# A fused diffusion step on one core: feed-forward in blocks of 128 inner columns with six PSUM banks for the down product, third modulation group summed on VectorE

## The reference, cut to what matters

```
D_MODEL = 1024; D_FF = 2816
def swiglu(h, w_gu, w_down):
    g, u = jnp.split(h @ w_gu, 2, axis=-1)
    return (jax.nn.silu(g) * u) @ w_down

x = x + g2 * swiglu(modulate(rmsnorm(x, norm2_g_0), s2, sc2), w_gu_0, w_down_0)
```

```
m = jax.nn.silu(cond.astype(F32)) @ w.astype(F32) + b.astype(F32)     # w: 1024 x 6144
```

## Time and profile before

| what | value |
|---|---|
| median of 3 runs | 1412.44 us (1411.51 to 1413.75) |
| profiled execution, first to last instruction (span) | 1408.6 us, which is 3.8 us under the median; no other time is given for it |
| PE / DVE / ACT busy | 96% / 79% / 58% of the span |
| mean granted TensorE clock | 0.986 of full speed |
| feed-forward, first gate matmul to last residual add | 254.4 to 539.9 us |

### The profile page before, as it was taken

How to read it: one execution, slowest core, us unless ns; L and a number is a source line. 1 busy time by engine, 2 the same in 40 slices (tenths; PEclk the granted TensorE clock), 3 DMA queues, 4 the chain that set the end, 5 groups by cost and what they waited for, 6 DMA issues and landing times.

```text
span 1408.6 us, 17000 instructions
## 1 busy us (share of the span) xinstructions
PE 1351.2 (96%) x6717; PEld 1126.3 (80%) x6717; DVE 1117.5 (79%) x1031; ACT 811.1 (58%) x812; POOL 238.1 (17%) x338
## 2 busy tenths in 40 slices
PE   4999989999999998989999999999999999999996
PEld 2787557799999986788888888888888888888884
DVE  2698766567676656658899899998998999989997
ACT  4432764423232224255777777777777777767773
POOL 4000681000000013001999200000000000000001
PEclk9999999999999999989999999999999999999998
DMA  9967444854554437537899999999999999999991
GB/s 312 378 228 268 134 144 163 312 196 151 180 179 163 166 147 245 196 135 290 288 401 388 363 412 371 381 388 355 414 375 372 412 348 397 386 355 406 369 413 53
DMA packets 119238, 409.75 MB, mean 291 GB/s; under 512 B 8385, under 2 KB 31090, under 8 KB 102258
## 3 DMA queue, kind: packets, MB, share of 16 engines
q1 hardware_dynamic: 111376, 382.24, 72.2%
q0 software_dynamic: 6704, 23.14, 5.4%
q10 hardware_dynamic: 1074, 3.23, 0.6%
HBM read 398.58 MB, written 9.99 MB: 290 GB/s over the span
## 4 chain that ended last, share of the span: by engine, by line
PE 88%; POOL 4%; DVE 3%; DMA 2%; ACT 1%; issue 1%; SPq 1%; POOLq 0%; DVEq 0%; ACTq 0%
PE ps L1814 26%; PE ps L1816 26%; PE ps L1815 26%; DMA raw<-in_ada_w 2%; PE ps L2196 1%; POOL xn L725 1%; POOL o_rstd L723 1%; DVE ring_lo L1612 1%; PE ps L2096 1%; POOL o_msq L721 1%; PE ps L2038 1%; PE ps L2139 1%; SPq L502 1%; PE ps L2169 1%; DMA gbc<-in_cache_v 0%
## 5 line engine op out<-in xcount | busy, mean ns | idle before, releaser
L1612 DVE TENSOR_TENSOR ring_lo<-raw,ring_hi 128x2048 fp32r<-128x2048 f32 (+1 forms) x210 | 451.9, 2168 | 49.2 <-ACT ring_hi L1048 48.5
L1048 ACT ACTIVATE ring_hi<-raw 128x2048 fp32r<-128x2048 f32 (+1 forms) x210 | 381.3, 1820 | 123.8 <-PE ps L1816 122.8
L1814 PE MATMUL ps<-ring_hi,xe 128*128 128x512 f32 x536 | 212.1, 396 | 1.3 <-DVE xe L1663 0.8
L1816 PE MATMUL ps<-ring_lo,xe 128*128 128x512 f32 x536 | 209.8, 391 | 0.0
L1815 PE MATMUL ps<-ring_hi,xe 128*128 128x512 f32 x536 | 209.3, 390 | 0.0
L824 ACT ACTIVATE ring_hi<-raw 128x2048 fp32r<-128x2048 f32 x52 | 99.3, 1914 | 168.3 <-PE ps L1816 156.1
L1192 DVE TENSOR_TENSOR ring_lo<-raw,ring_hi 128x2048 fp32r<-128x2048 f32 x52 | 118.2, 2288 | 83.6 <-ACT ring_hi L824 83.4
L1612 DVE TENSOR_TENSOR ring_lo_more<-raw,ring_hi_more 128x2048 fp32r<-128x2048 f32 (+1 forms) x70 | 151.8, 2168 | 16.7 <-ACT ring_hi_more L1048 16.5
L1048 ACT ACTIVATE ring_hi_more<-raw 128x2048 fp32r<-128x2048 f32 (+1 forms) x70 | 127.3, 1819 | 40.1 <-PE ps L1816 39.7
L1814 PEld LDWEIGHTS ps<-ring_hi,xe 128*128 128x128 f32 x536 | 101.4, 189 | 21.9 <-DVE xe L1663 0.9
L1816 PEld LDWEIGHTS ps<-ring_lo,xe 128*128 128x128 f32 x536 | 101.0, 188 | 21.5
(11 more groups left out here) (325 smaller groups left out, 2428.8 us busy)
## 6 DMA issues: line engine op xcount, KB each, us to landing
raw<-in_w_gu_e SPq DMA_DIRECT2D x128, 1024.0 KB, 8.1
raw<-in_w_down_e SPq DMA_DIRECT2D x88, 1024.0 KB, 9.0
raw<-in_w_gu_e SPq DMA_DIRECT2D x64, 768.0 KB, 6.9
raw<-in_ada_w SPq DMA_DIRECT2D x40, 1024.0 KB, 5.5
raw<-in_w_gu SPq DMA_DIRECT2D x44, 512.0 KB, 4.9
raw<-in_w_qkv SPq DMA_DIRECT2D x12, 1024.0 KB, 8.1
raw<-in_w_down SPq DMA_DIRECT2D x11, 1024.0 KB, 5.2
raw<-in_ada_w SPq DMA_DIRECT2D x16, 512.0 KB, 13.6
```

The lines of the kernel that those rows point to most:

```text
L1048: act.activation(ehi[m % RINGM][:, 0:w], raw[:, (MOE_U0 + m) % RAW, 0:w], ACT.Copy).then_inc(hi_ready, 1)
L1612: dve.tensor_tensor(elo[m % RINGM][:, 0:w], raw[:, (MOE_U0 + m) % RAW, 0:w], ehi[m % RINGM][:, 0:w].bitcast(F32), ALU.subtract).then_inc(l ...
L1814: pe.matmul(out, l_hi, r_hi, start=first, stop=False)
L1816: return pe.matmul(out, l_hi, r_lo, start=False, stop=last)
```

## The change

- The feed-forward goes in 22 blocks of 128 inner columns (`BLOCKS`). Two blocks share the three weight units of a chunk. A block's gate goes to bank 6 and its up to bank 7, 48 matmuls of 384 columns; then follows the down product of the block before, 18 matmuls of 512 columns.
- The six outputs of the down product have a bank each, 0 to 5, and are summed there over all 22 blocks. `add_y`, `yacc` and the 66 additions on DVE are gone; `add_gated` reads PSUM.
- PE must wait, before each block's gate and up, until DVE has read those of the block before (`ffh_ready`), and now works one down product of 18 matmuls in between.
- Group 3 is summed on DVE like groups 1 and 4 (`FOLDED`), in blocks 1 to 8, and group 4 in blocks 11 to 18 (`FOLD_FFN`). Their rows are summed on PE behind blocks 9 and 19, and turned behind 10 and 20. The `ada_unit` calls of group 3 are gone.
- `STREAM` and the split order on ACT and DVE follow the new order.

```diff
+BLOCKS = 2 * FFC
+FOLD_FFN = {1 + i: (3, i) for i in range(KC)} | {11 + i: (4, i) for i in range(KC)}
+SUM_AFTER = {9: 3, 19: 4}
+TURN_AFTER = {10: 3, 20: 4}
-FOLDED = (1, 4)
+FOLDED = (1, 3, 4)
...
+            for b in range(BLOCKS):                                    # ACT
+                c, at = b // 2, b % 2
+                if at:
+                    act.wait_ge(unit_used, FFN0 + 3 * c + 2)
+                else:
+                    act.wait_ge(gu_ps, c + 1)
+                if b >= 2:
+                    act.wait_ge(ffh_ready, b - 1)
+                act.activation(tnh[:, at, :], ps[:, 6, 0:TOK], ACT.Tanh, scale=0.5).then_inc(tanh_ready, 1)
+                act.wait_ge(ffh_ready, b + 1)
+                act.activation(ff_hi[:, at, :], hb[:, at, :], ACT.Copy).then_inc(ffhi_ready, 1)
+                if at == 0:
+                    split_hi(FFN0 + 3 * c + 2)
+                if c + 1 < FFC:
+                    split_hi(FFN0 + 3 * c + 3 + at)
...
+            for b in range(BLOCKS):                                    # DVE
+                c, at = b // 2, b % 2
+                dve.wait_ge(tanh_ready, b + 1)
+                link(dve.scalar_tensor_tensor(hb[:, at, :], tnh[:, at, :], 1.0, ps[:, 6, 0:TOK], ALU.add, ALU.mult))
+                dve.scalar_tensor_tensor(hb[:, at, :], hb[:, at, :], 0.5, ps[:, 7, 0:TOK],
+                                         ALU.mult, ALU.mult).then_inc(ffh_ready, 1)
+                dve.wait_ge(ffhi_ready, b + 1)
+                dve.tensor_tensor(ff_lo[:, at, :], hb[:, at, :], ff_hi[:, at, :].bitcast(F32),
+                                  ALU.subtract).then_inc(fflo_ready, 1)
+                if at and c + 1 < FFC:
+                    split_lo(FFN0 + 3 * c + 4)
+                if b in FOLD_FFN:
+                    fold_in(*FOLD_FFN[b])
+                if b in SUM_AFTER:
+                    ada_rows_out(SUM_AFTER[b])
+                if b in TURN_AFTER:
+                    ada_cols_out(TURN_AFTER[b])
+                if at == 0:
+                    split_lo(FFN0 + 3 * c + 2)
+                    if c + 1 < FFC:
+                        split_lo(FFN0 + 3 * c + 3)
...
-            turn_normed(1, lambda k: ada_unit(3, k) if k < 2 else None)
-            for k in range(2, KC - 2):
-                ada_unit(3, k)
+            turn_normed(1)
...
+            def add_down(b):
+                c, at = b // 2, b % 2
+                slot = (FFN0 + 3 * c + 2) % RING
+                pe.wait_ge(fflo_ready, b + 1)
+                pe.wait_ge(lo_ready, FFN0 + 3 * c + 3)
+                for k in range(TILES):
+                    cols = slice(k * P, (k + 1) * P)
+                    for half in range(2):
+                        w = slice(at * D + half * HALF, at * D + (half + 1) * HALF)
+                        ins = mm3(ps[:, 2 * k + half, :], ff_hi[:, at, cols], ff_lo[:, at, cols],
+                                  ring_hi[:, slot, w], ring_lo[:, slot, w], b == 0, b == BLOCKS - 1)
...
+            for b in range(BLOCKS):                                    # PE
+                if b:
+                    pe.wait_ge(ffh_ready, b)
+                    gate_up(b, 0)
+                gate_up(b, 1)
+                if b:
+                    add_down(b - 1)
+                if b in SUM_AFTER:
+                    pe.wait_ge(ffh_ready, b + 1)
+                    fold_unit(SUM_AFTER[b])
+                if b in TURN_AFTER:
+                    pe.wait_ge(ffh_ready, b + 1)
+                    ada_turn(TURN_AFTER[b])
+            add_down(BLOCKS - 1)
```

More of the change, by code:

```diff
@@ L97, in stream_before_experts @@
     s += wo[1:]
[L98 to L104, removed]
+    s += DENSE_UNITS[:2]
+    for b in range(BLOCKS):
+        c = b // 2
+        later = DENSE_UNITS[3 * c + 3:3 * c + 5]
+        fold = [("ada",) + FOLD_FFN[b]] if b in FOLD_FFN else []
+        s += later[1:] + fold if b % 2 else fold + [DENSE_UNITS[3 * c + 2]] + later[:1]
     s += [("ada", 5, k) for k in range(KC)]
@@ L115 @@
 FFN0 = WO0 + 4
-WF0 = FFN0 + NU
+WF0 = FFN0 + len(DENSE_UNITS)
 MOE0 = WF0 + 4
@@ L286, in dense @@
             with ExitStack() as q:
-                ff_hi = sb("ff_hi", [P, 2, 2, TOK], F32R, q)
-                ff_lo = sb("ff_lo", [P, 2, 2, TOK], F32R, q)
+                ff_hi = sb("ff_hi", [P, 2, TOK], F32R, q)
+                ff_lo = sb("ff_lo", [P, 2, TOK], F32R, q)
                 tnh = sb("tnh", [P, 2, TOK], F32, q)
@@ L2033, in _ @@
                     pe.wait_ge(hlo_ready, 12)
-                for q in range(4):
-                    for b in range(4):
-                        w = q * HALF + (b % 2) * 256 + (b // 2) * P
+                for up in range(2):
+                    for q in range(4):
+                        w = q * HALF + up * 256
                         for weight in weights:
-                            ins = pe.matmul(ps[:, b, 0:TOK], weight[:, FFN0 % RING, w:w + P], part[:, q, :],
-                                            start=(q == 0 and part is h_hi and weight is ring_hi), stop=False)
@@ new lines, in _, with gate_up @@
+                            pe.matmul(ps[:, 6 + up, 0:TOK], weight[:, FFN0 % RING, w:w + P], part[:, q, :],
+                                      start=(q == 0 and part is h_hi and weight is ring_hi), stop=False)
+            def gate_up(b, kh):
+                c, at = b // 2, b % 2
+                slot = (FFN0 + 3 * c + kh) % RING
+                pe.wait_ge(lo_ready, FFN0 + 3 * c + kh + 1)
+                for up in range(2):
+                    if up and kh == 0 and b - 1 in SUM_AFTER:
+                        pe.wait_ge(mrow_ready, SUM_AFTER[b - 1] + 2)
+                    if up and kh == 0 and b - 1 in TURN_AFTER:
+                        pe.wait_ge(modv_ready, TURN_AFTER[b - 1] + 2)
+                    for q in range(4):
+                        w = q * HALF + up * 256 + at * P
+                        ins = mm3(ps[:, 6 + up, 0:TOK], ring_hi[:, slot, w:w + P], ring_lo[:, slot, w:w + P],
+                                  h_hi[:, 4 * kh + q, :], h_lo[:, 4 * kh + q, :], kh == 0 and q == 0, kh == 1 and q == 3)
+                if at:
+                    ins.then_inc(unit_used, 1)
+                elif kh:
+                    ins.then_inc(gu_ps, 1)
```

120 lines of the change are left out of this document (22 added, 98 removed).

## The result

| | before | after |
|---|---|---|
| median | 1411.97 us (1410.95 to 1413.75, 4 runs) | 1419.54 us (1419.09 to 1420.38, 4 runs) |
| ratio | | 1.0053, interval 1.004 to 1.0066 |
| span of the profiled execution | 1408.6 us | 1417.6 us |
| mean granted clock | 0.986 | 0.979 |

The changed kernel is slower by 0.53%, 7.6 us by the medians and 9.0 us by the two spans. The forecast was 1416.6 us in a range from 1412.9 to 1420.8; the sign and the range held, and the time lies 2.9 us over the forecast. The kernel before came out at 1411.97 us here where the forecast had started from 1412.44, so as a difference the miss is larger: +7.6 us in place of +4.2, a little over the forecast's own upper bound of +7.2.

A forecast was written before the change was run, and what follows sets the result against it. The prediction took PE to bound the feed-forward, so relieving DVE saves nothing by itself. Its terms, +0.45 - 1.05 + 2.05 + 0 + 2.0 + 0.8 = +4.2 us on 1412.44, gave 1416.6 us, range 1412.9 to 1420.8.

The forecast's parts named there:

- gap behind the first block: Between the first two blocks, PE idles 2.0 us in place of 3.07, as the `ada_unit`s are gone: -1.05 us.
- `fold_unit(3)`: Group 3's row sum, new inside PE's chain in the feed-forward: 26.91 us a chunk against 24.86, +2.05 us.
- twice as many switches: PE changes between gate-and-up and down products twice as often: +0.45 us, at most 0.9.
- end of the feed-forward, without the clock: Behind the last down product, earlier last add (-0.1 to -0.4) set against PE free about 0.3 us late: 0.
- clock at the entrance: Before the first gate matmul, PE idles 5.4 us and then runs at its lower clock: +2.0 us (1.5 to 2.5).
- clock at the end: Behind the feed-forward, PE's gap grows from 2.88 to about 4.2 us; half the lower price of 1.5 to 2.5: +0.8.
- The bound: The feed-forward is bound by PE, busy 278.7 of 279.8 us; work leaving DVE gives no time back by itself.
- The schedule: Feed-forward blocks: 2.0 us idle between the first two, a tanh every 12.4 us, no other PE waits; +1.0 to +1.9.
- The clock holds: Rival: no added clock loss at the feed-forward's entrance or end, only schedule, 1413.4 to 1414.4 us; chance 0.26.
- A late split: Rival: PE stalls for late splits in odd blocks, +5, with the clock 1422 us; both kinds, about 1438; chance 0.12.
- A faster pitch: Rival: down product's 512-column pitch shrinks to 0.2133 us without DVE reading banks beside it, 1408.6 us; chance 0.06.

The follow-up runs named there:

- three gaps filled: Changed kernel plus unused identity transposes on idle PE: 36 at the feed-forward's entrance, 15 between the first two blocks, 30 at the end; 1.0017 of the kernel before.
- second trace of the changed kernel: The changed kernel profiled again with no edit; ratio 1.0039 to the kernel before, span 1414.0 us.
- blocks alone, filled: Changed kernel with group 3 back on PE, plus 15 unused transposes between the first two blocks and 30 at the end; 1.0004 of the kernel before.
- second trace of before: The kernel before profiled again with no edit; ratio 0.9999, span 1411.2 us.
- two gaps filled: Changed kernel plus unused identity transposes on idle PE, 36 at the feed-forward's entrance and 30 at its end; 1.0023 of the kernel before.
- a third kernel: Kernel before plus unused transposes: 16 before the first head's turn, 36 before the last attention output's, 24 at the feed-forward's end; 0.9986 of the kernel before.
- the kernel before with all places filled: Kernel before plus unused transposes at five places: 16, 36 and 24 as in the third kernel, 15 more at the feed-forward's entrance; ratio 0.9993.

## Why the prediction was right, and which term was off

Both columns are us against the kernel before. The measured ones for the schedule come from the traces of the changed kernel and of three gaps filled, where the clock was at full, and those for the clock from the first and second trace of the changed kernel less that one.

| step | predicted | measured |
|---|---|---|
| gap behind the first block | -1.05 | 1.92 - 3.07 = -1.15 |
| `fold_unit(3)` | +2.05 | (392.61 - 378.11) - 12.47 = +2.03 |
| twice as many switches | +0.45 (0 to 0.9) | +0.8, what is left of +1.70 |
| end of the feed-forward, without the clock | 0 | 11.86 - 11.89 = 0 |
| clock at the entrance | +2.0 (1.5 to 2.5) | +1.68 and +2.45 |
| clock at the end | +0.8 | 14.49 and 13.30 less 11.86: +2.6 and +1.4 |
| sum | +4.2 | +6.0 and +5.6 |

**The bound** was read rightly: 66 additions left DVE and no time came back (blocks alone, filled: 1.0004).

**The schedule** came out as worked: the gap is 1.92 us where 2.0 were said, a tanh follows every 12.47 us where 12.4 were, PE waits for nothing else, and the first residual multiply starts 540.66 - 538.21 = 2.45 us ahead of the end of the down product where before it was 534.02 - 527.48 = 6.54, 4.1 nearer; the last add ends 8.06 us behind it, like 12 operations. The switches cost near their upper bound: ACT's timeline shows 0.07 us a pair of blocks, which is 0.8 over eleven.

**The clock at the entrance** behaved as said, and filling the gap took its price away (1.67 us). How much it costs depends on the execution. The Trainium skill, "TensorE: Matmul & The Clock Gate", Part 1: The HAM clock gate, says that the number of slow matmuls differs between runs of one kernel; the two traces of the changed kernel agree, with 1.68 and 2.45 us.

**The clock at the end is the mis-sized term**: "I take half of the lower price, +0.8." The gap was right (4.07 for 4.2), but the halving was not: in all four traces in which the blocks' end stood unfilled the clock fell, for 1.4 to 2.6 us (11.86 the measure), and in neither trace of before did it. My reason for halving, that before might pay it already behind 2.88 us, has no trace for it at this place; at the first head the clock did fall behind gaps of 2.81 and 2.85 us, so the length of a gap alone does not tell. With the mean of the two traces of the changed kernel, 2.0, the forecast would have been 1417.8; the two comparisons gave +7.6 and +5.9 us by the medians (1418.67 - 1412.77 the second).

**What remains** is 0.3 to 1.6 us between the measured sums and the differences of the medians, and the close agreement of the second is partly luck: its trace is the shortest of five executions. There the feed-forward and the tail are 5.6 us over the second trace of before, but the span only 2.8, since the first gate came 1.03 us earlier and the stretch from Fourier to the experts was 1.65 us shorter. Three things that the runs showed can fill the rest, and I cannot divide it between them: the fall behind the first block (1.6 us in one of the traces), the chance ahead of the feed-forward, and the clock in the routing. The profiled execution of before was early by 2.5 us against the second one; I had set the median 3.8 us over its span, where the second trace has a device time of 1413.0 us for its span of 1411.2, only 1.8 more. The sum was made as a difference, so this did not move the forecast.

**The rivals.** *The clock holds*: refuted by the pitch of 0.32 at the entrance; in the lengths of stages it is what the filled kernels show, +1.7 where +1.0 to +1.9 was given. *A late split*: refuted, PE waits in no block but the second. *A faster pitch*: refuted by 0.2265.

## What to carry to other kernels

When work leaves the engine that sets the time, ask what the hole does to its clock: here a gap that costs nothing by the schedule, since PE waited anyway, cost 1.7 to 2.5 us behind it, and one that grew from 2.9 to 4.1 us cost as much again. Count a reason for a fall in full until a trace of the same gap says otherwise. And before one trace is set against another, run the unchanged kernel twice, and compare stage by stage: a third of the difference between the first two spans lay ahead of the change.

## What the runs showed of the hardware that I had not expected

- A gap near 1.8 us can already cost the clock, in some executions and not in others: it held behind 1.82 in two traces of before and fell behind 1.83 in a third kernel that is the same up to there but for its fillers; it held behind the first block in the changed kernel (1.76) and fell behind 1.75 with two gaps filled. It held behind 2.88 at the end of the feed-forward in both traces of before. At the first head, where shorter idle stretches follow, it fell behind 1.69, 2.27 and 2.85 and held behind 1.74 and 2.48, each in one trace. So no single length of gap divides the two cases in these traces.
- Unused transposes keep the clock up: at the attention's output the 24 transposes took 2.84 us behind 36 fillers, 4.34 without. They are no guarantee: behind 16 of them at the first head it fell in one of four traces (0.83 from 140 to 144 us).
- The load of the cached values took 6.9 to 9.2 us from issue to landing in the thirteen traces, in code that is the same.
- A busy PE is no guarantee of the clock. In the routing of the kernel before, PE is busy with 48 matmuls of 8 columns for 7.95 us from 608.95 on, and the windows from 612 to 621 us have a granted clock of 0.50. From the first of them to the first expert matmul it is 24.18 us there and 20.90 in the kernel before with all places filled, with 13.7 and 6.8 us at half clock.
